# Hybrid decoder layer on one Trainium2 core: the squared-key sums as two fp32r products, and three of VectorE's weight remainders moved

## The reference, cut to what matters

```python
def rwkv7_group(z, ...):                 # z: token-shifted projection, 528 tokens
    ...
    w = -softplus(-(w0 + tanh(wd) @ w2)) - 0.5
    decay = exp(-exp(w))
    a = sigmoid(a0 + ad @ a2)
    kk = heads(k * k_k)
    kk = kk / maximum(norm(kk, axis=-1, keepdims=True), 1e-12)
    k = k * (1.0 + (a - 1.0) * k_a)
    y = wkv7_scan(r, decay, k, v, -kk, kk * a)       # per head of 64 features
    bonus = sum(r * k * r_k, axis=-1, keepdims=True) * v
    ...                                              # group norm of y, + bonus, gate
def reference(...):
    p = rms_norm(h) @ w_in                           # 2048 -> 6432 columns
    y = concat([short_conv_group(p[:3072]), rwkv7_group(shift(p[3072:]))]) @ w_out
    h = h + y
    h = h + square(relu(rms_norm(h) @ w_up)) @ w_down
    return rms_norm(h)[16:]
```

## Time and profile before

| | us |
|---|---|
| median of 3 runs | 2428.42 |
| lowest, highest | 2427.71, 2428.54 |
| the profiled execution's own time | 2427.97 |
| its span, first to last instruction | 2426.1 |
| TensorE busy with matmuls | 2401.2 |
| VectorE busy | 1130.0 |
| ScalarE busy | 787.9 |
| GpSimd busy | 206.5 |

### The profile page before, as it was taken

One profiled execution on the slowest core, in us unless ns is written; L12 is line 12 of the kernel. 1 busy time (PEld: TensorE's weight loads), 2 busy tenths in 40 slices (PEclk: granted clock), 3 DMA queues, 4 the chain that ended last, 5 costly groups with the idle time before them and its releaser, 6 DMA issues.

```text
span 2426.1 us, 42112 instructions
## 1 busy us (share of the span) xinstructions
PE 2401.2 (99%) x16524; PEld 2034.1 (84%) x16524; DVE 1130.0 (47%) x1733; ACT 787.9 (32%) x1329; POOL 206.5 (9%) x249
## 2 busy tenths in 40 slices
PE   8999999999999999999999999999999999999997
PEld 8999999999998788888888888888888888888886
DVE  7557657657657644433333333333332333333343
ACT  6534434434434322322222222221322322222333
POOL 6101101001002322000000000000000000000032
PEclk9999999999999999999999999999999999999998
DMA  8344244244244632333233333333332332332232
GB/s 248 81 98 103 68 101 103 69 105 101 70 102 116 190 107 79 96 105 96 82 110 92 90 97 96 88 105 87 87 108 84 99 101 84 100 104 87 87 100 92
DMA packets 487454, 243.68 MB, mean 100 GB/s; under 512 B 83294, under 2 KB 481120, under 8 KB 486880
## 3 DMA queue, kind: packets, MB, share of 16 engines
q1 hardware_dynamic: 470064, 219.99, 32.8%
q0 software_dynamic: 6720, 18.45, 2.4%
q10 hardware_dynamic: 10496, 2.62, 0.6%
HBM read 224.08 MB, written 16.92 MB: 99 GB/s over the span
## 4 chain that ended last, share of the span: by engine, by line
PE 89%; DVE 7%; ACT 1%; issue 1%; DMA 1%; SPq 0%; ACTq 0%; DVEq 0%
PE PD L1512 68%; PE PD L1517 13%; PE PD L1728 1%; DVE uni L1160 1%; DVE uni L1286 1%; DVE w_lo L1065 1%; PE PD L1541 1%; PE PW L1541 1%; PE PW L1690 1%; PE PW L1590 0%; PE PD L1446 0%; PE PW L1595 0%; DVE uni L1164 0%; PE PW L1654 0%; PE PW L1696 0%
## 5 line engine op out<-in xcount | busy, mean ns | idle before, releaser
L757 ACT CAST w_hi<-w_raw 128x512 fp32r<-128x512 f32 x780 | 457.6, 620 | 700.8 <-PE PD L1512 525.7
L1065 DVE TENSOR_TENSOR w_lo<-w_raw,w_hi 128x512 fp32r<-128x512 f32 x780 | 548.5, 736 | 293.0 <-ACT w_hi L757 289.8
L1512 PE MATMUL PD<-act_lo,w_hi 128*128 128x512 f32 x1344 | 531.3, 395 | 0.0
L1512 PE MATMUL PD<-act_hi,w_hi 128*128 128x512 f32 x1344 | 529.1, 394 | 0.0
L1512 PE MATMUL PD<-act_hi,w_lo 128*128 128x512 f32 x1344 | 528.6, 393 | 0.0
L1512 PE MATMUL PD<-u_hi,w_hi 128*128 128x512 f32 x1024 | 409.7, 400 | 0.0
L1512 PE MATMUL PD<-u_hi,w_lo 128*128 128x512 f32 x1024 | 403.3, 394 | 0.0
L1512 PE MATMUL PD<-u_lo,w_hi 128*128 128x512 f32 x1024 | 401.5, 392 | 0.0
L1512 PEld LDWEIGHTS PD<-act_hi,w_hi 128*128 128x128 f32 x1344 | 252.5, 188 | 61.7 <-issue 1.4
L1512 PEld LDWEIGHTS PD<-act_lo,w_hi 128*128 128x128 f32 x1344 | 252.1, 188 | 58.3 <-issue 0.2
L1512 PEld LDWEIGHTS PD<-act_hi,w_lo 128*128 128x128 f32 x1344 | 252.8, 188 | 57.3
(11 more groups left out here) (319 smaller groups left out, 1880.5 us busy)
## 6 DMA issues: line engine op xcount, KB each, us to landing
w_raw<-in_w_up SPq DMA_DIRECT2D x256, 256.0 KB, 3.2
w_raw<-in_w_down SPq DMA_DIRECT2D x256, 256.0 KB, 2.9
w_raw<-in_w_in SPq DMA_DIRECT2D x200, 256.0 KB, 3.1
w_raw<-in_w_out SPq DMA_DIRECT2D x64, 256.0 KB, 2.7
residual<-res POOLq DMA_DIRECT2D x2, 2048.0 KB, 10.1
out<-rows SPq DMA_DIRECT2D x8, 512.0 KB, 5.3
yin<-mixed POOLq DMA_DIRECT2D x15, 256.0 KB, 3.6
x_rows<-in_x SPq DMA_DIRECT2D x3, 1024.0 KB, 7.4
```

The lines of the kernel that those rows point to most:

```text
L757: nc.scalar.copy(w_hi[:, q % RING], w_raw[:, q % RAW]).then_inc(hi_split, 1)
L1065: V.tensor_tensor(w_lo[:, q % RING], w_raw[:, q % RAW], w_hi[:, q % RING].bitcast(F32), ALU.subtract).then_inc(lo_split, 1)
L1512: ins = M(pd_seq(n), w, v[:, k, first:first + SEQ], start=begin, stop=end)
```

## The change

**The sums.** `square_keys` on ScalarE now also copies `fsq` into `k_sq_hi`, rounded to fp32r; GpSimd subtracts it from `fsq` into `k_sq_lo` (`split_squares`). Step ss of TensorE sums both with the rounded matrix `same_head_r`: two halves of the high part, two of the low part, into the same PSUM columns. The matrix `same_head` goes. The squares of the next pair are made in step var ahead of the root of the variance, and no longer behind it.

**The remainders.** VectorE's count of quarters is held back by two at vtr, and by one at the end of a pair (ahead6); the next pair makes that one up behind its own step ss. ScalarE's casts and the loads keep their places in their lists.

```diff
@@ gpsimd
+        def split_squares(j):
+            pool.wait_ge(k_sq_rounded, j + 1)
+            nc.gpsimd.tensor_tensor(k_sq_lo[:], fsq, k_sq_hi[:].bitcast(F32), ALU.subtract).then_inc(k_sq_split, 1)
...
             else:
+                split_squares(j + 1)
                 pool.wait_ge(dve_done, step(DVE_STEPS, "y4", j))
...
         load_g(0)
+        split_squares(0)
@@ scalar
         def square_keys(j):
             act.wait_ge(z_done, at(5, 3, j))
             nc.scalar.activation(fsq, zk[:], ACT.Square, scale=p_("k_k", j)).then_inc(k_squared, 1)
+            act.wait_ge(k_squared, j + 1)
+            nc.scalar.copy(k_sq_hi[:], fsq).then_inc(k_sq_rounded, 1)
...
                 if name == "var":
+                    if not last:
+                        square_keys(j + 1)
                     pe("var")
                     done("std", nc.scalar.activation(ysq, PW[:, 0, :], ACT.Sqrt, bias=eps_t[:, 1:2]))
-                if name == "ahead6" and not last:
-                    square_keys(j + 1)
@@ vector
-            splits, tiles, y_split = 0, 0, 0
+            splits, tiles, y_split = -1 if j else 0, 0, 0
...
-                while splits < (96 if last and name == "var" else k - 4 if last and name in ("amv", "ahead5") else k) // KQ:
+                held = 2 if name == "vtr" else 1 if name == "ahead6" and not last or last and name in ("amv", "ahead5") else 0
+                while splits < (96 if last and name == "var" else k) // KQ - held:
                     split(Q_PAIR + LEAD + splits, 24, j)
@@ tensor
                 if name == "ss":
-                    pe.wait_ge(k_squared, j + 1)
-                    for a in range(2):
-                        ins = M(PW[:, 2 + a, 0:HALF], same_head[:], half(fsq, a), start=True, stop=True)
+                    for i, (made, squares) in enumerate(((k_sq_rounded, k_sq_hi), (k_sq_split, k_sq_lo))):
+                        pe.wait_ge(made, j + 1)
+                        for a in range(2):
+                            ins = M(PW[:, 2 + a, 0:HALF], same_head_r[:], half(squares[:], a), start=(i == 0), stop=(i == 1))
```

More of the change, by code:

```diff
@@ L196 @@
 T_END = T_MLP + FFG * 24
-N_CONST = 4 + 6 + 4 + 5 + 3 + 4 + 2
+N_CONST = 4 + 6 + 4 + 4 + 3 + 4 + 2
 def hybrid_layer(nc, x, meta, norm_mix_g, w_in, shift_mu, conv_w, decay_w0, decay_w2, iclr_a0, iclr_a2,
@@ L232, in hybrid_layer @@
     ones = sb("ones", [P, P])
-    same_head = sb("same_head", [P, P])
     same_head_r = sb("same_head_r", [P, P], F32R)
@@ L262, in hybrid_layer @@
     KA = m_sb("KA", [P, 2, SLOTS, 2, C])
+    over_pairs = ExitStack()
+    k_sq_lo = sb("k_sq_lo", [P, T], F32R, on=over_pairs)
+    over_pairs.close()
     AMV = m_sb("AMV", [P, 2, SLOTS, P])
@@ L292, in hybrid_layer @@
     over_states.close()
+    over_last_states = ExitStack()
+    k_sq_hi = sb("k_sq_hi", [P, T], F32R, on=over_last_states)
+    over_last_states.close()
     ZB = m_sb("ZB", [P, 7, P])
@@ L358, in hybrid_layer @@
     z_done, k_squared, key_made = sem("z_done"), sem("k_squared"), sem("key_made")
+    k_sq_rounded, k_sq_split = sem("k_sq_rounded"), sem("k_sq_split")
     conv_step = sem("conv_step")
@@ L571, in _ @@
                 const(nc.gpsimd.tensor_tensor(level_mask[hs, i, :], blocks[hs, i + 1, hs], blocks[hs, i, hs], ALU.subtract))
-        const(nc.gpsimd.tensor_copy(same_head[:], blocks[:, 2, :]))
         const(nc.gpsimd.tensor_copy(same_head_r[:], blocks[:, 2, :]))
```

## The result

| | before | after |
|---|---|---|
| median, us | 2428.79 | 2435.12 |
| lowest to highest | 2427.23 to 2429.66 | 2431.19 to 2436.63 |
| runs | 13 | 13 |
| profiled execution's span | 2426.1 | 2429.6 |

The ratio is 1.0023, with a 95% interval of 1.0016 to 1.0030: the change makes the kernel slower by 6.3 us. The forecast was 3.8 us slower. The time lies in the range given, at its upper end, and over the 2434 that was named for the forecast and (a) alone. Because 6.3 is over the 4.9 us that were called measurable, it falls on the side "slower" (which had 0.27) and not on "within" (0.60).

The account below looks back on a forecast made before the run. TensorE, busy 99% of the span, was taken as the bound, with GpSimd's late subtraction setting pairs after the change. First pair -0.4, seven others +0.6 each: +3.8 us, from 2428.42 to a median of 2432.2; range 2422 to 2436.

Parts of the forecast that it names:

- upper end: 2436: GpSimd's later mask products block VectorE's remainder, second Gram mask some 0.2 us late, +1.4 in all, 2433.6, and some.
- (a): Same late load, but GpSimd's subtraction goes ahead of VectorE's second remainder: pair longer by 0.2 us, +1.0, 2429.4; chance 20%.
- slower: Outcome slower than before by more than the measurable 0.2%, 4.9 us, from 0.76 us a pair; chance 0.27.
- within: Outcome that a measurement can't tell from no change, within 0.2%, 4.9 us; chance 0.60.
- The sums: TensorE's key sums: four fp32r products take 0.49 us where two fp32 ones took 0.89, saving 0.4 a pair; feeding costs nothing.
- The old waits: TensorE's waits at Gram, transposes and bonus sum (0.15, 0.21, 0.06), 0.42 us a pair from the second on, used up.
- The late load: Moved remainder frees its raw buffer later, delaying load, ScalarE's cast and rounding, GpSimd's subtraction and bonus sum, which starts at 210.2.
- (b): Bonus sum not late at all: full gain of 6.1 us, 2422.3; chance 18% with all between it and no change.
- The turns of VectorE and GpSimd: Ahead of the bonus sum, VectorE's second remainder starts 0.15 us before GpSimd's subtraction, which takes about 1.7 us, not 1.28.
- (c): Load lands later, three being issued within 1.3 us: at 4.2 us after issue +12.2, 2440.6; chance 18%.
- mis-sized term: Each pair from the second on longer by 0.6 us, sums' 0.4 and old waits' 0.42 already used up; seven times.
- rival (d): The four products of the sums cost 0.89 us as before, so only the first pair loses its gain: +4.2, 2432.6; 4%.

Follow-up runs that it names:

- two repeats: The changed kernel, nothing altered, profiled a second and third time, one execution each: 2432.96 and 2433.19 us, against 2427.16 for the kernel before.
- version without the first move: Changed kernel with bonus rounding ahead of ScalarE's casts and a pair's last remainder back ahead of the key-sum maximum: 2423.65 us, ratio 0.9981 to the kernel before.
- best version: Changed kernel, but in step gram0 ScalarE rounds the bonus operand ahead of its two weight casts: 2423.43 us against 2428.55 before, ratio 0.9979.

## Why the prediction was right, and what it missed

**The sums**: forecast 0.49 us in place of 0.89, measured 0.48; the first pair gained 0.42 for a forecast 0.4. Their feeding cost nothing, as said: the rounding copy takes 0.63, GpSimd is done at 181.35, three microseconds ahead of TensorE.

**The old waits**: the Gram 19.34 and the transposes 22.87 us behind the sums, forecast 19.4 and 22.9. All 0.42 went.

**The late load**: step by step as forecast, if one counts from the key sums, which come 0.46 earlier. Load issued 19.39 behind the sums (forecast 204.18 - 184.81 = 19.37), cast at 22.46 (22.38), GpSimd at 23.68 (23.64), bonus sum in effect at 25.4 (25.4); the pair 92.44 (92.4). The version with the rounding first shows that this chain is the cause: without it the full gain of rival (b) is there. Its last bonus sum stands 5.7 us ahead of that of before, where (b) had 6.1 for the whole kernel; its median is 5.1 lower, since TensorE waits more behind it (below).

**The turns of VectorE and GpSimd**: the row of L657 says 1.58 us, 1.74 at the longest, where it said 1.28; in the forecast "about 1.7". The version with one remainder fewer puts their price at 0.31 to 0.47 us a pair, of the 0.4 between "about 1.7" and 1.28. Rival (a), GpSimd first, happened too, in the third pair:

```profile
298.99 0.62 ACT L768 CAST w_hi<-w_raw 128x512 fp32r<-128x512 f32 x1 [3.99 <-DMA w_raw<-in_w_in]
299.64 2.39 DVE L1077 TENSOR_TENSOR w_lo<-w_raw,w_hi 128x512 fp32r<-128x512 f32 x2
300.22 1.26 POOL L657 TENSOR_TENSOR rb_lo<-uni,rb_hi 128x512 fp32r<-128x512 f32 x1 [16.61 <-ACT rb_hi L892]
301.54 0.51 PE L1612 MATMUL PW<-rb_hi,same_head_r 128*128 128x512 f32 x1 [0.56 <-POOL rb_lo L657]
```

Now VectorE's second remainder is the one that is stretched (2.39 for two and not 1.29), `rb_lo` takes its 1.26, and the pair 91.86, as (a) says: 0.06 longer than before, where it had put 0.2. The Trainium skill, "SBUF — State Buffer", section "SBUF: two separate sides", says that the lock goes to whoever starts first and is kept for the whole instruction; both kinds of pair agree, and 0.58 us hangs on a start that differs by a tenth. Against (a) stood that rows repeat to a few hundredths in all pairs. VectorE's do here, but the load is ready 2.81 us behind its issue in this pair and 2.92 in the next three, and that is the tenth.

**The landings**: the seventh pair takes 93.00. Its load is issued at 665.35 and the cast can start only at 669.30, 3.95 us later; in the eighth it is 4.34. This is rival (c), in two pairs of eight and not in all. The same distance is 2.81 to 3.07 in the five pairs ahead, and 2.91 to 3.06 in all seven in the kernel before. The two repeats have 3.70 and 4.11, 4.31 and 4.14 in these pairs.

The traces show what these late loads have in common. Besides the loads of weights the DMA engines carry transfers that the profile calls `instruction`, of 16 KB and about 1 us each. One falls into the seventh pair's load, from its issue to its landing (`--dma`, window 665.35:669.27; queue, packets, MB, share):

```profile
665.35 4.55 SPq L457 DMA_DIRECT2D w_raw<-in_w_in  x4
669.30 0.63 ACT L768 CAST w_hi<-w_raw 128x512 fp32r<-128x512 f32 x1 [5.12 <-DMA w_raw<-in_w_in]
```

```profile
q8 instruction: 1, 0.02, 1.8%
```

In the same stretch of the second pair (203.74:206.8) none begins. The one shown begins at 666.28, 0.93 us behind the issue of the load, that of the eighth pair 1.45 behind. Over all fourteen profiles and eight pairs, that is 112 such loads: in 15 a transfer of this kind begins 0.88 to 1.45 us behind the issue, and these 15 land 3.67 to 4.32 us after it. Of the other 97, 95 land within 3.54; the two left are the seventh and eighth pair of the version without the first move, 4.71 and 4.68, with such a transfer 2.5 us behind the issue. In the kernel before none comes at that distance. Rival (c) had put the lateness down to the three loads together; they are issued as close in the pairs where nothing is late. No run moves these transfers alone, so that they are the cause isn't shown.

So the profile of after adds up to its last bonus sum: forecast 3.8; 0.04 more in each ordinary pair, +0.2; the third pair -0.6; seventh and eighth +1.5; together 4.9, and it starts 765.2 - 760.4 = 4.8 later than before. The stretch from there to the end is 1664.4 us in this profile and 1665.7 in that of before (1667.0 in that of the best version), which leaves the 3.5 of the spans. A good part of these differences are waits of TensorE for VectorE in the rest of the eighth pair: 1.4 us before, 0.5 in after, 2.0 in the best version. The three lists (before, after, best version), from behind the last bonus sum to 830 us:

```profile
PE PD L1728 <- DVE act_lo L1133: 0.9, 2, 0.5
PE PW L1624 <- DVE uni L1258: 0.3, 1, 0.3
...
```

```profile
PE PD L1742 <- DVE act_lo L1145: 0.5, 1, 0.5
```

```profile
PE PD L1742 <- DVE act_lo L1145: 1.3, 2, 0.8
PE PW L1638 <- DVE uni L1270: 0.7, 1, 0.7
```

The forecast let a gain or a loss in the pairs pass through to the end in full. It does not quite: what these waits are differs from version to version, by up to 1.5 us.

**The mis-sized term** is the price of a pair's lateness: "longer by 0.6 us" seven times. It took all pairs to be alike and each late microsecond to cost one. First, late landings come in some pairs only, the seventh and eighth, and there the waits reach 1.4 to 2.1 us. Second, a fall of the granted clock can stand behind such a wait and cost 1.5 us more. A fall of the clock stood nowhere in the forecast; the kernel before has no such wait in its pairs, and no row of it shows one there. The median is 6.3 and not 3.8 us over before, and two of the three profiles of after have one fall of the clock, 1.5 us each. So the chain and the length of an ordinary pair were foreseen. That the time still lies in the range is owed to its upper end, set for another reason, GpSimd's mask products holding up the second Gram mask. In the profile of after TensorE waits for no such mask: between 93 and 830 us its only waits are the seven for `rb_lo`, 8.9 us, and one of 0.5 for VectorE's `act_lo`. And that the first profile's span fits the sum as well as it does, 3.5 against 3.8, is in part luck: two pairs longer than forecast, one shorter, and fewer waits behind them cancel.

**What stays open.** That the instruction transfers make the loads late is a pattern in all the traces, not a result of an experiment; the same three loads are issued within 1.2 to 1.6 us in every pair from the second on. Which part of the median is the clock and which the landings isn't shown either, since the other runs have a time and a mean clock, but no trace; one to three falls a run would cover the 3.7 us between the shortest runs and the median. That the moves alone (2431.26, waits up to 1.3, clock at 1.00) and the whole change (2435.12) differ by 3.9 us with pairs of the same length fits the clock, and is no proof of it. Nor is it known why one wait of about 2 us, or of 1.74, leaves the clock up and another brings it down.

## What to carry to other kernels

An instruction that gives a buffer back is also the start of a load. Before it is moved, follow the load, the engine that waits for it, and everything that stands behind that wait in the engine's list: here a rounding that needed nothing of the load stood there, and putting it ahead turned a loss of 6.3 us into a gain of 5.1. A gain on TensorE is kept only while the next operand has room for it, so read how far ahead of need each operand is ready before the sum is made. The waits of about a microsecond cost their length here; some from 1.74 us on brought the clock down, which in the pairs cost 1.5 us on top.

## What the runs showed of the hardware

- TensorE's granted clock can fall in a kernel in which it is 99% busy: to 0.50, the lower level, for some 3 us behind single waits of 1.86, 2.05, 2.47, 3.04 and 3.05 us, at 1.5 us for each fall in the pairs. Behind 1.88, 2.08 and 2.24 it stayed at 1.00, and so it did behind the waits for `rb_lo` of 0.2 to 1.8 us, 38 of them. Behind the wait of 1.74 or 1.75 in the opening stage it fell in two profiles of fourteen.
- A subtraction of 128 x 512 on GpSimd takes 1.26 to 1.30 us alone and 1.50 to 1.76 (three profiles of after) when VectorE's remainder of two SBUF operands has started 0.04 to 0.31 us ahead; if GpSimd is first, VectorE's two take 2.39 and not 1.29.
- A load of a quarter is ready for its cast 2.8 to 3.2 us after issue in the first six pairs of the three profiles of after, and 3.7 to 4.3 in the last two. In all fourteen profiles, the 15 loads at this place behind whose issue a 16 KB `instruction` transfer begins within 0.88 to 1.45 us land after 3.67 to 4.32 us.
